# Narrower position-bias units, first weight split on GpSimd, earlier x, in a fused two-block transformer kernel

## The reference

```python
mod = silu(c) @ w_ada[l] + b_ada[l]
sh1, sc1, g1, sh2, sc2, g2 = split(mod, 6)
h = x * (1.0 + sc1) + sh1
proj = h @ w_in[l]
...
bias = rel_bias[t5_bucket(q_pos - k_pos)]
logits = q @ k * a_scale + bias
logits = where(key <= query, logits, -inf)
```

## Time and profile before

| what | value |
|---|---|
| median of three runs | 2335.96 us |
| profiled execution | 2338.04 us |
| its span in the trace | 2336.1 us |
| TensorE busy | 2299.2 us, 98% |
| VectorE, ScalarE, GpSimd busy | 53%, 43%, 43% |
| first matmul of slot 0 | 45.48 us from the start |
| first matmul of slot 1 | 57.27 us |

### The profile page before, as it was taken

One profiled execution on the slowest core, in us unless ns is written; L12 is line 12 of the kernel. 1 busy time (PEld: TensorE's weight loads), 2 busy tenths in 40 slices (PEclk: granted clock), 3 DMA queues, 4 the chain that ended last, 5 costly groups with the idle time before them and its releaser, 6 DMA issues.

```text
span 2336.1 us, 32099 instructions
## 1 busy us (share of the span) xinstructions
PE 2299.2 (98%) x11346; PEld 1852.5 (79%) x11346; DVE 1245.9 (53%) x2649; ACT 995.3 (43%) x1665; POOL 994.1 (43%) x892
## 2 busy tenths in 40 slices
PE   7999999999999999999999999999999999999998
PEld 4778878888888877887788888888888877788767
DVE  8665766844435357568476344315630163286674
ACT  7454455344433244545524344423142354333473
POOL 3432223544544453313245445445554434445472
PEclk9999999999999999999999999999999999999999
DMA  9642144322226354313442222223222311222210
GB/s 354 233 131 71 54 130 145 124 96 102 90 79 246 108 199 144 98 45 101 132 178 73 98 100 90 87 99 115 96 90 90 108 77 38 89 91 90 91 46 37
DMA packets 52644, 260.60 MB, mean 112 GB/s; under 512 B 6640, under 2 KB 16368, under 8 KB 26928
## 3 DMA queue, kind: packets, MB, share of 16 engines
q1 hardware_dynamic: 51376, 250.68, 31.2%
q0 software_dynamic: 1152, 8.39, 0.9%
HBM read 249.47 MB, written 7.34 MB: 110 GB/s over the span
## 4 chain that ended last, share of the span: by engine, by line
PE 81%; issue 10%; POOL 4%; DVE 3%; ACT 2%; DMA 1%; SPq 0%; POOLq 0%; DVEq 0%; ACTq 0%
PE bank L754 23%; PE bank L756 22%; PE bank L755 22%; POOL w_lo L612 4%; PE bank L1009 3%; PE bank L917 1%; PE bank L1014 1%; PE bank L1273 1%; PE bank L906 1%; PE bank L1051 1%; PE bank L892 1%; DMA ada_early<-w_ada 1%; PE bank L1262 1%; PE bank L1427 1%; PE bank L869 0%
## 5 line engine op out<-in xcount | busy, mean ns | idle before, releaser
L612 POOL TENSOR_TENSOR w_lo<-w_raw,w_hi 128x512 fp32r<-128x512 f32 (+2 forms) x732 | 878.0, 1231 | 1159.4 <-ACT w_hi L1479 774.7
L754 PE MATMUL bank<-h_hi,w_hi 128*128 128x512 f32 x1616 | 645.6, 399 | 0.8 <-POOL w_lo L612 0.8
L756 PE MATMUL bank<-h_hi,w_lo 128*128 128x512 f32 x1616 | 630.5, 390 | 0.0
L755 PE MATMUL bank<-h_lo,w_hi 128*128 128x512 f32 x1616 | 629.6, 390 | 0.0
L754 PEld LDWEIGHTS bank<-h_hi,w_hi 128*128 128x128 f32 x1616 | 304.0, 188 | 67.2 <-issue 8.2
L756 PEld LDWEIGHTS bank<-h_hi,w_lo 128*128 128x128 f32 x1616 | 303.3, 188 | 64.6
L755 PEld LDWEIGHTS bank<-h_lo,w_hi 128*128 128x128 f32 x1616 | 304.0, 188 | 58.7 <-issue 1.0
L1479 ACT ACTIVATE w_hi<-w_raw 128x2048 fp32r<-128x2048 f32 (+2 forms) x108 | 189.9, 1758 | 274.4 <-PE bank L756 253.5
L2375 DVE SCALAR_TENSOR_TENSOR cv<-bank,par,cv 128x511 f32<-128x511 f32 (+1 forms) x176 | 131.7, 749 | 214.6 <-ACT cv L1746 200.2
L1484 ACT ACTIVATE w_hi<-w_raw 128x2048 fp32r<-128x2048 f32 x68 | 129.8, 1909 | 125.6 <-PE bank L756 117.1
L1746 ACT ACTIVATE cv<-bank,par 128x512 f32<-128x512 f32 x88 | 68.4, 779 | 233.4 <-PE bank L756 232.0
(11 more groups left out here) (378 smaller groups left out, 3794.3 us busy)
## 6 DMA issues: line engine op xcount, KB each, us to landing
w_raw<-w_stream SPq DMA_DIRECT2D x150, 1024.0 KB, 4.9
w_raw<-w_down SPq DMA_DIRECT2D x32, 704.0 KB, 4.0
ada_mid<-w_ada SPq DMA_DIRECT2D x20, 1024.0 KB, 5.6
ada_last<-w_ada SPq DMA_DIRECT2D x12, 1024.0 KB, 4.9
ada_early<-w_ada POOLq DMA_DIRECT2D x8, 1024.0 KB, 15.2
ada_late<-w_ada SPq DMA_DIRECT2D x8, 1024.0 KB, 6.5
bias_in<-bias_scratch SPq DMA_DIRECT2D x16, 256.0 KB, 3.0
bias_in<-bias_scratch SPq DMA_DIRECT2D x16, 192.0 KB, 2.7
```

The costliest lines, as they stand in the source:

```text
L612: ins = nc.gpsimd.tensor_tensor(w_lo[r][:, part], w_raw[r][:, part], w_hi[r][:, part].bitcast(fp32), ALU.subtract)
L754: nc.tensor.matmul(out, w[0][:, cols], xh, start=first, stop=False)
L755: nc.tensor.matmul(out, w[0][:, cols], xl, start=False, stop=False)
L756: return nc.tensor.matmul(out, w[1][:, cols], xh, start=False, stop=last)
```

## The change

- `seen(G)` = 16 (G + 1) replaces n in steps, sign, the products and out: a unit is computed only up to the key of its last query. The store still writes 128 (i + 1) columns.
- The columns behind `seen(G)` of each stage tile are set to zero on GpSimd (`clear_tails`): 21 tiles of blocks 0 to 2 right behind the eight loads, 7 tiles of block 3 behind w_lo of slot 0, with a wait for ada_row. Their widths are 112, 96, ... 16 columns in each block. SP waits for them (tails_clear) ahead of the stores.
- w_hi of slot 0 is copied by GpSimd in four pieces of 512 columns, between the first clears and w_lo of slot 0; the copy on ScalarE is gone. ScalarE waits for w_hi_done ahead of its w_hi of slot 1.
- x is loaded when ada_early 5 has landed (before: 6). Slot 1, and with it everything queued behind it on SP, waits for x to land.
- The products of the modulation, its row copies and column products stand behind later units; h_hi(0) and h_hi(1) stand behind unit 30, and ada_take behind the steps of unit 31.

```diff
-        ADA_AFTER = (8, 9, 11, 13, 16, 18, 21, 24)
+        ADA_AFTER = (9, 10, 12, 15, 17, 20, 24, 27)
+
+        def seen(G):
+            return 16 * (G + 1)
...
-            sp.wait_ge(ada_first[6], 16)
+            sp.wait_ge(ada_first[5], 16)
             sp.dma_start(x[:, :, :], a["x"]).then_inc(x_loaded, 16)
             sp.wait_ge(ada_first[7], 16)
+            sp.wait_ge(x_loaded, 16)
             weights(0, 1, a["w_stream"][0, 1])
             for i, G in BIAS_UNITS:
                 n = (i + 1) * P
+                sp.wait_ge(tails_clear, 1 + i // 3)
                 sp.wait_ge(bias_out, G + 1)
...
+            def clear_tails(blocks):
+                for i, G in BIAS_UNITS:
+                    if i in blocks and seen(G) < (i + 1) * P:
+                        ins = nc.gpsimd.memset(stage[G][:, seen(G):(i + 1) * P], 0.0)
+                ins.then_inc(tails_clear, 1)
+
+            clear_tails(range(3))
+            pool.wait_ge(w_full[0], 16)
+            for at in range(0, SLOT, 512):
+                ins = nc.gpsimd.tensor_copy(w_hi[0][:, at:at + 512], w_raw[0][:, at:at + 512])
+            ins.then_inc(w_hi_done, 1)
             lo(slot_no(0, 0))
+            pool.wait_ge(ada_row, 3)
+            clear_tails((3,))
             lo(slot_no(0, 1))
...
-                if G in (12, 17, 22):
-                    ada_columns((12, 17, 22).index(G))
-                if G == 27:
+                if G in (13, 18, 23):
+                    ada_columns((13, 18, 23).index(G))
+                if G == 29:
                     ada_columns(3).then_inc(ada_sum, 1)
...
-                if G in (10, 14, 19, 25):
-                    half = (10, 14, 19, 25).index(G)
+                if G in (11, 16, 21, 28):
+                    half = (11, 16, 21, 28).index(G)
...
-                if G == 21:
-                    split_hi(0, 0)
-                if G == 29:
+                if G == 30:
                     act.wait_ge(x_loaded, 16)
                     act.wait_ge(ada_mod, 1)
                     for j in range(2):
...
                         if j == 3:
+                            act.wait_ge(w_hi_done, 1)
                             split_hi(0, 1)
...
                 steps(G)
-                if G == 29:
+                if G == 31:
                     dve.wait_ge(par_loaded, 16 * 4)
                     ada_take(0, 0)
```

More of the change, by code:

```diff
@@ L291, in build @@
         bias_out = sem("bias_out")
+        tails_clear = sem("tails_clear")
         bias_stored = [sem(f"bias_stored{i}") for i in range(NB)]
@@ L807, in bias_unit @@
             def bias_unit(i, G):
-                n = (i + 1) * P
+                n = seen(G)
                 bank = banks[BIAS_BANKS[G % 4]]
@@ L1498, in sign @@
             def sign(G):
-                n = (G // 8 + 1) * P
+                n = seen(G)
                 if G >= 4:
```

## The result

| what | before | after |
|---|---|---|
| median, runs on the same chips (20 each) | 2337.86 us | 2341.19 us |
| profiled span | 2336.1 us | 2337.6 us |
| end of VectorE's unbroken steps (before to unit 29, after to unit 31) | 36.75 | 43.45 |
| first matmul of slot 0 | 45.48 | 48.51 |
| first matmul of slot 1 | 57.27 | 59.93 |

The ratio is 1.0013, with a 95% interval of 1.0007 to 1.0019. That is +3.0 us, from +1.6 to +4.4, and within the 0.3% that the prediction called no change. The forecast was +2.4. Ratios are of fast executions alone: one of the 20 of the kernel before (4642.74 us) and two of the 13 of e_only_narrow (3274.32 and 6257.53) stood far off and are not in them.

What follows compares the result with a forecast made beforehand. ScalarE's bias units, its w_hi copy and an odd VectorE delay were taken to bound the stage before slot 0. A later start (+1.1) and the clock (+1.3) gave +2.4 on 2335.96: 2338.4 us, range 2333.0 to 2342.5.

Steps and rivals of the forecast that it cites:

- The stage, its path and the stake: Ahead of the first projection slot: without GpSimd it could start at 41.2, 4.3 us sooner, and the end would shift equally.
- ScalarE's saving: Bias units on ScalarE: narrower sign and out save 3.0 us; the moved w_hi copy saves 1.8 more.
- The two exclude each other, and an unbroken row of steps holds GpSimd off to its end: VectorE's steps keep GpSimd waiting, so copies follow 36.8 and w_lo is ready at 46.6, starting slot 0 1.1 us later.
- rival A: GpSimd gets in between steps; slot 0 starts at 41.2, slot 2 waits behind the stores; gain 1.6 us, 2334.4; chance 0.24.
- VectorE's end at 36.8: VectorE's 32 narrower units end at about 36.8, where 30 wide ones ended at 36.75.
- Prices of clear and copy: GpSimd: 0.15 us a clear; 0.87 a copy, so 3.5 for four; seven clears left after the gaps cost 1.05.
- the lower bound: With copies of 0.48 and clears of 0.10, slot 0 starts at 43.9 and slot 2 binds: -0.1 us.
- The clock: TensorE idles 6.5 us before slot 0, whose half clock then costs 2.15 instead of 0.9 us: 1.3 more.
- a sign that it is wrong: The forecast fails if VectorE has long gaps after 27, or if h_hi releases the start of slot 0.
- x, stores and slot 2: SP's queue: x lands at about 36, stores begin at 37.9, 29 take 17.5; slot 2 is hidden with 1.0 us to spare.
- B: Full gain: as rival A, but faster stores or early slot 2 don't bind; -4.3 us, 2331.7; chance 0.06.
- C: Slower: gaps admit no clear, clears and copies cost upper bounds, w_lo ready at 53.2; +9.0 us, 2345.0; chance 0.10.

Runs made afterwards that it cites:

- e_only_narrow: Kernel before with narrow units alone, clears of blocks 0 to 2 at the head of GpSimd's queue, block 3 ahead of w_lo; 2337.24 us, ratio 0.9995.
- v_best: Kernel after, first clears at queue head, w_hi of slot 0 on ScalarE, w_lo behind VectorE's last step, no wait for x; 2335.26 against 2336.61 us.
- e_hi_act: Kernel after with w_hi of slot 0 copied by ScalarE again, behind unit 21; 2336.22 against 2337.02 us, ratio 0.9993.
- e_copies_late: Kernel after with GpSimd's four copies and w_lo of slot 0 waiting until VectorE's last step is done; 2337.77 us, ratio 1.0002.
- v_best_x: v_best with the wait of slot 1 and the stores for x kept; 2336.80 us, ratio 0.9996 to the kernel before.
- e_only_copies: Kernel before with w_hi of slot 0 copied early by GpSimd instead of ScalarE, units wide, nothing cleared; 2338.99 us, ratio 1.0006.
- e_wide: Kernel before with four clears, four w_hi copies and w_lo on GpSimd beside VectorE's wide steps, ScalarE's copy out; 2338.73 us in one execution.

## Why the prediction was right or wrong

**The stage, its path and the stake: right.** All of the change lies ahead of slot 1, and the shift there goes on to the end. v_best reached 42.25 for slot 0, where "the first slot could start at 41.2" had been worked out. Its last row copy began at 37.45 (forecast 37.2) and h_hi(0) ended at 41.36 (41.1); the missing 1.0 is w_lo, which there waits for the steps. But the 3.0 us of ScalarE's saving are not a sum that any kernel gets: with the products in their old places 0.7 was left of them (e_only_narrow).

**"The two exclude each other, and an unbroken row of steps holds GpSimd off to its end": this is the step that failed.** It was drawn from the first line of the earlier trace rows alone, a two-input piece beside steps of 512 keys. It holds for that case in three kernels (the first piece waited 3.1 us before, 4.9 in e_hi_act, 2.6 in e_only_narrow), and not for clears or copies, nor for pieces that directly follow them. With it fell the forecast of clears in groups inside gaps, of copies behind 36.8, and of w_lo at 46.6; measured: 9.72, 11.60, 18.98.

**The other way round was left out.** The prediction read from the earlier trace rows that a step of 0.43 took 1.44 beside a piece, and from the earlier trace rows that three steps took 1.2 too long, used both as proof of exclusion, and put no price on them in the forecast or in rival A, which let GpSimd in between the steps for nothing. The trace had the price: about 1 us for each of four pieces, and by the same reasoning a copy's length for each of four copies, 4.0 + 3.5 = 7.5 with the prediction's own price of a copy and 4.0 + 2.3 = 6.3 with the measured one, before the clears. Measured, from the ends of the steps: 43.45 after, 41.94 without the clears beside them, 37.80 with the clears but without copies and w_lo, 37.12 in v_best without any of them. So copies and w_lo cost 4.8 alone and 5.65 on top of the clears, the clears 0.7 alone, and all together 6.3. That this is the 6.3 of the estimate is chance, since the estimate leaves the clears out. VectorE had no slack at small widths, which the prediction itself said.

**VectorE's end at 36.8: right without GpSimd** (37.12 in v_best). Forecast and kernel differ by 6.65, the 6.3 above and the 0.3 of the forecast.

**Prices of clear and copy: too high.** In a row, 1.96 / 21 = 0.09 a clear (taken: 0.15, bounds 0.10 to 0.29) and 2.28 / 4 = 0.57 a copy (taken: 0.87, bounds 0.48 to 1.26). Each was set toward the wrong row: the clear lay at its lower bound and the copy near the small two-input piece. With the measured prices and the clears out of the way the forecast's own course would start slot 0 at 36.8 + 2.3 + 5.05 + 0.2 = 44.4, and e_copies_late, with steps to 37.80, started it at 45.29, where 46.6 had been forecast. In the lower bound a sum is off: 36.8 + 4 x 0.48 + 5.05 + 0.2 is 44.0, and 43.5 with one of the four copies in a gap, not 43.9; it changes nothing in the range. A sentence on the page cited there: 769 ns, by the Trainium skill (GPSIMD Engine Reference, section 3.1), is for a tight loop over 512 elements, and the 0.57 of these copies lies below it.

**The clock: near for its own course in one execution, wrong for this one.** Behind 3.2 us of idle time, and with the clock at half since about 40, the slot took 13.5 (e_copies_late; forecast 13.05 behind a longer idle time). In the kernel after TensorE came to the slot from bias units that ran right ahead of it, and the slot took 11.4. Start and clock erred in opposite ways: 46.6 + 13.05 = 59.65 forecast, 48.51 + 11.42 = 59.93 measured. The total was met by luck, for a reason that was not the one given: w_lo was ready at 18.98 and had no part in the start, and h_hi released the slot, which the prediction had named as a sign that it is wrong.

**x, stores and slot 2.** x landed at 36.6 (36) and the stores began at 37.1 (37.9), but x released them, the clears had long been done. The 29 stores took 15.8, not the 17.45 that was called "SP's own rate"; of the slow issues of before (1.32 and 1.38 us, and a row of 0.6 to 0.8) only one came again (1.62). Slot 2 was loaded by about 60 and did not bind, because slot 0 was late; in v_best_x, where slot 0 is early, it does, as rival A had it.

**The rivals.** B's size was met at slot 1 by another kernel (v_best, 4.0) in one execution, 2.3 of it by the clock; v_best_x, with the wait for x kept, had 1.2. A was half right: GpSimd got in, and slot 0 was not at 41.2 for it. C's size and course did not occur. Missing was the case that came: GpSimd gets in and VectorE is what stands, and the delay reaches h_hi(0) over ScalarE.

**What stays open.** Why the 21 clears and the 4 copies behind them hold VectorE for their whole length, three steps of 4.0 to 4.3 us (2.07 beside the clears alone in e_copies_late), while the copies of e_only_copies and e_wide alternate with steps one for one. And why a two-input piece that arrives alone is held off where a copy is not; whether it is so beside narrow steps was not tried. Both are observations of these kernels, without a cause shown. The Trainium skill, SBUF — State Buffer, section "SBUF: two separate sides", has the pair of ports held for the whole instruction by whoever starts first: the one-for-one rows agree with it, while neither the 4.29 us step nor a piece that waits through 8 steps or more follows from it.

## What to carry to other kernels

Where two engines exclude each other, price both directions from the trace, and ask which of the two has slack: here work was moved from ScalarE to an engine with time to spare, and paid for by a third that had none. A row that shows A waiting for B does not say that A always loses; look for the row that shows B waiting. Put such work where the critical engine has ended its own (one wait, and w_lo behind the last step), or ahead of its start, as the clears at the head of the queue. What that was worth here is small: the ratio of v_best is 0.999 (0.9981 to 0.9999). And a saving on an engine counts only from where it stops waiting: in e_only_narrow ScalarE still waited for the loads of w_ada, and 0.7 of 3.0 us were left.

## What the hardware showed beyond the question

The granted clock dips at a few places far behind the change, in some executions and not in others; the mean granted clock of the executions of the kernel before lies between 0.996 (2341.97 us) and 1.000 (2335.0 us). Windows of 8 us of the kernel before, near 806, 1245 and 2250 us:

```profile
804.00:812.00 8.00, 8.00 (x53) 7.21 (x52) 4.73 (x11) 3.05 (x4) 3.48 (x3) 1.00 0.45 142
1243.00:1251.00 8.00, 7.84 (x36) 5.59 (x35) 7.55 (x11) 6.05 (x10) 8.00 (x7) 1.00 0.00 0
...
2248.00:2256.00 8.00, 7.04 (x33) 4.79 (x34) 4.92 (x17) 5.56 (x20) 6.38 (x12) 0.79 0.01 2
```

and of v_best:

```profile
804.00:812.00 8.00, 8.00 (x38) 6.89 (x38) 3.27 (x9) 1.52 (x3) 3.39 (x3) 0.79 0.41 133
1243.00:1251.00 8.00, 8.00 (x31) 6.42 (x31) 7.38 (x12) 5.38 (x9) 8.00 (x8) 0.83 0.00 0
```

A mean of 0.79 over 8 us is 3.4 us at half clock. Laid side by side with the matmuls of a trace that lacks the dip, what follows is shifted by 1.6 us behind 806 (3.2 in e_hi_act), 1.2 behind 2236 (v_best), 1.7 behind 2250, and only 0.3 to 0.4 behind 1245. Together that is as much as this whole change. So a shift of a few us is read from the two streams of matmuls laid side by side, right behind the change, and a span or a single run does not show it. Even there the clock has its part, as slot 0 of v_best and v_best_x shows. The few executions with a mean granted clock of 1.000 leave it out: 2335.0 for the kernel before, 2334.08 for v_best, 2337.98 to 2338.36 for e_only_copies, by the rounding of three digits and on different chips.
